# Seven units of an expert table fetched ahead of the first pass, and ten row products in the query stage

## The chip, the cores and the metric

The kernel runs as one program on 1 core of a Trainium2 chip. The metric is device time in microseconds (us), the median over runs; less is better. The kernel is written by hand for each engine: TensorE (PE, weight loads PEld), VectorE (DVE), ScalarE (ACT), GpSimd (POOL) and SyncE (SP). Each runs its own list of instructions in order and waits on semaphores. Transfers (DMA) are issued by SP, ACT and POOL on a queue each, and all run on the same 16 DMA engines.

## The reference

One layer of a transformer block on 256 tokens of width 2048, float32: a normalised input is projected (`w_in`), two attentions run beside each other, their outputs go through `w_o`, and then comes the part that this change is about:

```python
x = x + concat(A, B) @ w_o
h = rmsnorm(x)
qr = (h @ w_pq).reshape(b, t, 8, 2, 128)
sc = einsum('bthpd,hpnd->bthpn', qr, sub_keys)
s_top, i_top = top_k(sc, 16)
cand = s_top[..., 0, :, None] + s_top[..., 1, None, :]
c_top, c_pos = top_k(cand, 16)
expert = i0 * 128 + i1
a = gelu(einsum('bthkd,btd->bthk', u_tab[expert], h))
x = x + einsum('bthk,bthkd->btd', softmax(c_top) * a, v_tab[expert])
```

Each token picks 8 x 16 of 16384 experts; an expert is a row of 2048 numbers in the first table (`u_tab`) and one in the second (`v_tab`).

## The kernel before, in words

**Two ways of computing the experts.** The 128 later tokens take the dense way: TensorE multiplies all of `u_tab` in 128 units of 128 experts (1 MB each) with the tokens (`u_chunk`, L1597), the first pass; the results are gated by what each token picked, and a second pass multiplies them with the 128 units of `v_tab` (`v_chunk`, L1643). The 128 earlier tokens take the sparse way: for each of 128 picks POOL gathers one row of the table for each token (128 rows of 8 KB, 1 MB; "a row" below is such a gather) and VectorE multiplies it with the tokens (L1192) or adds it up weighted (L1201). There are 256 rows, first 128 of `u_tab`, then 128 of `v_tab`; gathers of the second table skip what has no weight.

**Stages, on the profile's clock.** Input projection and attentions to about 347 us; the output projection `w_o` in two groups of 16 loads, the second from about 350 to 408; the query stage (`w_pq`, 32 loads) to about 509; the first pass to 1016; the second pass to the end.

**Weights in two parts.** In the stages up to the queries each load of 0.5 MB comes into one of four raw buffers (SP, `load`, L383). ScalarE rounds its two halves (`split_hi`, L570), VectorE subtracts to get the low part of each half (`split_lo_half`, L877), and TensorE multiplies both parts. Four halves can be ahead of TensorE; a raw buffer is loaded again when its low parts are made. In the query stage a half is a low part of 128 x 512, there are 64, and TensorE's products with it are L1538, L1539 and L1543.

**Units of the first table.** Five units (0 to 4) are loaded by SP in the query stage, one after every fourth weight load (`first_unit`, L418), into places of `acts` that are free by then. The others go through a ring of four buffers: the even ones by SP (L436 to L446), the odd ones by ScalarE (`odd_unit`, L816), each when the unit that lay there has been used (`unit_used`). In the first pass the sums of a chunk go to ScalarE for the gelu (L783).

**Rows.** POOL's `gather(r)` (L525, L527) waits until the row's buffer has been used (`row_used`). The first `R_FRONT` = 8 rows turn through two buffers in the query stage; then there are six, from `R_MORE` on eight. `pool.memset` (L536) fills the place where gates will lie with ones; it waits until five units have been used, because units lie there, and the gathers behind it wait with it. VectorE's order is written out by hand: after the first head's `top_k` it makes four low parts, then a row product (L1241 to L1246); then the other heads with two rows each; in the gated half one row for each second chunk. The gate operands (`hots`, L1261) come behind the 46th row.

**Second pass.** Units 0 to 5 are loaded whole, the others gathered by POOL (L544) when the unit six before has been used, skipping experts that nobody used. After unit u POOL gathers rows up to `end`, a straight line over the units (L546). At the end VectorE makes the last row in four pieces (L1199), and adds up the outputs (L1350).

Of the kernel before, what the change touches and what calls it, by code (L numbers as in the profile page):

```python
# [18 lines left out]
def build_block(nc, io):  # L19
# [5 lines left out]
    ACT = mybir.ActivationFunctionType  # L25
# [43 lines left out]
    NRING, NROW = 4, 8  # L69
# [7 lines left out]
    with ExitStack() as ctx:  # L77
# [101 lines left out]
        x2n = [region(D * b, D) for b in range(TT)]  # L179
        A_QR = TT * D  # L180
        qr = region(A_QR, 16 * SEQ).rearrange("p (c t) -> p c t", c=16)
# [6 lines left out]
        first_units = [region(2 * UNIT * i, 2 * UNIT) for i in (0, 1, 4, 7, 5)]  # L188
# [60 lines left out]
        first_in = [sem(f"first_in{i}") for i in range(NRING + 1)]  # L249
# [94 lines left out]
        ROWS_U = 88  # L344
        R_FRONT, R_MORE, ROWS_PICKED = 8, 46, 39
# [5 lines left out]
        ROWS_SB = 81  # L351
# [24 lines left out]
        def _(sp):  # L376
# [26 lines left out]
            wo = io["w_o"].rearrange("(k p) n -> p k n", p=P)  # L403
            for group in range(2):
                with sp.Fori(0, D // 512) as n:
                    for j in range(4):
                        k = 8 * group + 2 * j
                        load(n * 4 + (B_WO + 16 * group + j), j, wo[:, k:k + 2, ds(n * 512, 512)])
            def u_unit(v):
                return io["u_tab"][ds(v * P, P), :]  # L410
# [6 lines left out]
            def first_unit(j):  # L417
                sp.dma_start(first_units[j], u_unit(j)).then_inc(first_in[j], 16)  # L418

            query_weights(0, 3)  # L420
            sp.wait_ge(piece_used, 2 * B_PQ + 2)
            first_unit(0)
            query_weights(3, 4)
            first_unit(1)
            query_weights(4, 5)
            first_unit(2)
            query_weights(5, 6)
            first_unit(3)
            query_weights(6, 7)
            sp.wait_ge(x2_stored, 16)  # L430
# [123 lines left out]
        def _(act):  # L554
# [1165 lines left out]
```

## Time and profile before

| what | value |
|---|---|
| median of 3 runs | 1521.25 us (1520.91 to 1523.61) |
| the profiled execution's own time | 1521.85 us |
| its span, first to last instruction | 1519.8 us |
| busy: TensorE, weight loads | 96%, 72% |
| busy: VectorE, ScalarE, GpSimd | 76%, 32%, 28% |
| moved by DMA | 516.25 MB, mean 340 GB/s |

A busy share is an average over stages with different limits: TensorE is near its pace everywhere, while the DMA engines are full in the later two thirds alone. So what one step costs is read from its own stretch: who was waited for there, and how long. Rows of a timeline give the start, the duration, engine, line, operation and tiles, how many were merged (x), and in brackets the idle time before and what ended it.

### The profile page before, as it was taken

The numbers are of one execution on the slowest core, as the hardware profiler recorded it, in microseconds if no ns is written. First come the engines' busy times: TensorE is split into PE (matmuls) and PEld (weight loads), VectorE is DVE, ScalarE is ACT, GpSimd is POOL, SyncE is SP. The second block draws the span as 40 slices with busy tenths as digits, with TensorE's granted clock in tenths as the row PEclk, the third lists the DMA queues.
The fourth block names the chain that finished last, engine by engine and source line by source line (L and its number), as shares of the span: only waits on it lengthen the run. The fifth ranks groups of instructions, "written<-read, shape, count | busy, mean of one in ns | idle before, by whom it ended". The sixth has DMA issues, their size and how long they took to land.

```text
span 1519.8 us, 21779 instructions
## 1 busy us (share of the span) xinstructions
PE 1451.8 (96%) x7977; PEld 1099.0 (72%) x7977; DVE 1154.4 (76%) x1797; ACT 487.8 (32%) x1402; POOL 430.5 (28%) x422
## 2 busy tenths in 40 slices
PE   8999999999999999999989999998897899999998
PEld 6767888888899999999989999983333343444443
DVE  5425688586687799999377777778766899998997
ACT  6646656764655200000134444457000000000000
POOL 2020000000001232222210111126444666665762
PEclk9999999999999999999999999999989999999999
DMA  9764544637669899999999999999999999999997
GB/s 348 277 139 111 163 134 139 206 131 240 205 232 407 335 398 422 421 422 421 422 421 421 422 422 416 403 414 417 419 416 417 404 392 398 398 412 352 382 408 281
DMA packets 115528, 516.25 MB, mean 340 GB/s; under 512 B 26112, under 2 KB 28288, under 8 KB 63312
## 3 DMA queue, kind: packets, MB, share of 16 engines
q0 software_dynamic: 57776, 294.93, 49.0%
q1 hardware_dynamic: 47888, 154.09, 27.9%
q10 hardware_dynamic: 9792, 66.35, 10.6%
q8 instruction: 35, 0.57, 0.2%
q14 instruction: 37, 0.30, 0.1%
HBM read 628.91 MB, written 3.41 MB: 416 GB/s over the span
## 4 chain that ended last, share of the span: by engine, by line
PE 53%; DMA 23%; DVE 16%; issue 4%; POOL 3%; ACT 1%; another core or an unknown queue 0%; POOLq 0%; ACTq 0%; SPq 0%; DVEq 0%
PE ps L1643 12%; PE ps L1597 12%; DMA acts<-in_v_tab,acts 8%; PE ps L1379 6%; PE ps L1384 6%; PE ps L1381 6%; DMA late<-in_u_rows,sel 6%; DVE late L1192 3%; DMA raw<-in_v_tab,acts 3%; DMA late<-in_v_tab,acts 3%; DVE ps L1201 2%; PE ps L1401 2%; PE ps L1543 2%; PE ps L1539 2%; PE ps L1538 2%
## 5 line engine op out<-in xcount | busy, mean ns | idle before, releaser
L877 DVE TENSOR_TENSOR w_lo<-raw,w_hi 128x512 fp32r<-128x512 f32 (+1 forms) x288 | 188.1, 682 | 129.7 <-ACT w_hi L570 127.7
L1597 PE MATMUL ps<-acts,late 128*128 128x128 f32 x1984 | 233.4, 277 | 7.3 <-DMA late<-in_u_tab 6.0
L1597 PEld LDWEIGHTS ps<-acts,late 128*128 128x128 f32 x1984 | 227.6, 193 | 10.8 <-ACT acts L783 5.7
L1597 PE MATMUL ps<-acts,raw 128*128 128x128 f32 x1952 | 228.7, 276 | 5.3 <-DMA raw<-in_u_tab 3.7
L1597 PEld LDWEIGHTS ps<-acts,raw 128*128 128x128 f32 x1952 | 222.1, 192 | 9.0 <-DMA raw<-in_u_tab 4.4
L570 ACT ACTIVATE w_hi<-raw 128x512 fp32r<-128x512 f32 (+1 forms) x288 | 170.2, 622 | 85.3 <-PE ps L1543 40.3
L1643 PE MATMUL ps<-raw,acts 128*128 128x512 f32 x352 | 161.8, 611 | 13.1 <-DMA raw<-in_v_tab,acts 10.7
L1643 PE MATMUL ps<-acts 128*128 128x512 f32 x336 | 156.9, 618 | 16.7 <-DMA acts<-in_v_tab,acts 15.5
L1201 DVE SCALAR_TENSOR_TENSOR ps<-acts,sel,ps 128x2048 f32<-128x2048 f32 x63 | 148.4, 2355 | 16.8 <-DMA acts<-in_v_tab,acts 9.4
L1201 DVE SCALAR_TENSOR_TENSOR ps<-late,sel,ps 128x2048 f32<-128x2048 f32 x63 | 148.4, 2355 | 15.2 <-DMA late<-in_v_tab,acts 7.9
L1643 PE MATMUL ps<-late,acts 128*128 128x512 f32 x336 | 150.3, 597 | 9.8 <-DMA late<-in_v_tab,acts 8.5
L1379 PE MATMUL ps<-w_hi,hT_hi 128*128 128x512 f32 (+1 forms) x448 | 148.9, 413 | 3.9 <-DVE hT_lo L890 3.2
L525 POOL DMA_INDIRECT acts<-in_u_rows,sel x62 | 72.8, 1174 | 265.7 <-DVE acts L1192 213.4
L525 POOL DMA_INDIRECT late<-in_u_rows,sel x66 | 79.2, 1199 | 238.5 <-DVE late L1192 218.4
L1643 PEld LDWEIGHTS ps<-raw,acts 128*128 128x128 f32 x352 | 67.4, 195 | 104.3 <-issue 83.1
L1643 PEld LDWEIGHTS ps<-acts 128*128 128x128 f32 x336 | 64.8, 197 | 106.0 <-issue 78.3
L1384 PE MATMUL ps<-w_lo,hT_hi 128*128 128x512 f32 (+1 forms) x448 | 137.5, 388 | 0.6 <-DVE w_lo L877 0.6
L1381 PE MATMUL ps<-w_hi,hT_lo 128*128 128x512 f32 (+1 forms) x448 | 137.7, 389 | 0.0
L1643 PEld LDWEIGHTS ps<-late,acts 128*128 128x128 f32 x336 | 62.3, 190 | 95.6 <-issue 74.3
L1192 DVE SCALAR_TENSOR_TENSOR late<-late,acts 128x2048 f32<-128x2048 f32 x43 | 97.7, 2287 | 26.8 <-DMA late<-in_u_rows,sel 26.6
L1379 PEld LDWEIGHTS ps<-w_hi,hT_hi 128*128 128x128 f32 x448 | 80.8, 190 | 25.2 <-issue 6.8
L1384 PEld LDWEIGHTS ps<-w_lo,hT_hi 128*128 128x128 f32 x448 | 84.2, 188 | 18.2 <-DVE w_lo L877 1.1
(225 smaller groups left out, 1958.0 us busy)
## 6 DMA issues: line engine op xcount, KB each, us to landing
raw<-in_w_in SPq DMA_DIRECT2D x72, 512.0 KB, 4.2
late<-in_u_tab SPq DMA_DIRECT2D x32, 1024.0 KB
raw<-in_u_tab SPq DMA_DIRECT2D x31, 1024.0 KB
raw<-in_u_tab ACTq DMA_DIRECT2D x30, 1024.0 KB
late<-in_u_tab ACTq DMA_DIRECT2D x30, 1024.0 KB
raw<-in_w_o SPq DMA_DIRECT2D x32, 512.0 KB, 4.3
raw<-in_w_pq SPq DMA_DIRECT2D x32, 512.0 KB, 4.7
acts<-in_u_tab SPq DMA_DIRECT2D x5, 1024.0 KB, 8.8
```

Of the source, the lines that this page charges most:

```text
L525: pool.indirect_dma_start(row[BUF[r]], None, io["u_rows"], bass.IndirectOffsetOnAxis(ap=idx[:, n:n + 1], axis=0)).then_inc(row_in[BUF[r]], 16)
L570: nc.scalar.activation(whi[(2 * j + half) % NPART][:, 0:w], raw[j % NRAW][:, half * w:half * w + w], ACT.Copy).then_inc(hi_done, 1)
L877: V.tensor_tensor(wlo[slot_no][:, 0:w], raw[j % NRAW][:, half * w:half * w + w], whi[slot_no][:, 0:w].bitcast(F32), ALU.subtract).then_inc ...
L1192: V.scalar_tensor_tensor(row[BUF[r]], row[BUF[r]], 1.0, held if moved else hs, ALU.mult, ALU.mult, accum_out=a_sel[:, n:n + 1]).then_inc(r ...
L1201: V.scalar_tensor_tensor(held, row[BUF[r]], w_sp[:, n:n + 1], acc if r == V_ROW[0] else held, ALU.mult, ALU.add).then_inc(row_used, 1)
L1379: mm(out[b], hT_hi[:, k, t[b]], whi[part][:, 0:w], start=start and kk == 0, stop=False)
L1381: mm(out[b], hT_lo[:, k, t[b]], whi[part][:, 0:w], start=False, stop=False)
L1384: ins = mm(out[b], hT_hi[:, k, t[b]], wlo[part][:, 0:w], start=False, stop=stop and kk == 1)
L1401: ins = mm(ps[:, bank, :], src[:, k, b * P:b * P + P], w[:, k, :], start=k == 0, stop=k == ks - 1)
L1538: mm(out, whi[piece % NPART][:, w], hT_hi[:, k, :], start=k == 0, stop=False)
L1597: ins = mm(ps[:, q, 0:N_DN], unit[:, k * P:k * P + P], hF[:, k, :], start=k == 0, stop=k == KD - 1)
L1643: ins = mm(out_bank(n), acts_c[i * V_FULL + q], ring[q][:, 512 * n:512 * n + 512], start=first, stop=last)
```

## The change

Seven units instead of five are loaded ahead. Units 0 to 4 go out in the second half of `w_o`: SP waits for the last value products (`y_mm`), then issues unit 0, and one more behind every fourth weight load. Units 5 and 6 follow in the query stage, where unit 6 waits for a copy that lay in its place. Units 8 and 9 go to the ring as soon as the raw buffers under it are free, 7 and 10 at the end of the stage. The room comes from the queries, which are now kept in a ring of four small places instead of 16, and from the squares' output, which is moved. The fill with ones waits for seven used units. VectorE makes three low parts between two row products instead of four, so ten rows instead of eight lie in the query stage, and all marks that count rows move by two. In the second pass the straight line for the rows is divided by 123 and not by 120, so that it no longer reaches the last row before the last unit.

```diff
-    NRING, NROW = 4, 8
+    NRING, NROW, N_FIRST = 4, 8, 7
...
-        x2n = [region(D * b, D) for b in range(TT)]
-        A_QR = TT * D
-        qr = region(A_QR, 16 * SEQ).rearrange("p (c t) -> p c t", c=16)
+        x2n = [region(A_HF + D * b, D) for b in range(TT)]
+        qr = [early[:, 256:512], early[:, 1024:1280], early[:, 1408:1664], gate_low[:, 0:SEQ]]
...
-        first_units = [region(2 * UNIT * i, 2 * UNIT) for i in (0, 1, 4, 7, 5)]
+        first_units = [region(2 * UNIT * i, 2 * UNIT) for i in (0, 1, 2, 3, 4, 7, 5)]
...
-        ROWS_U = 88
-        R_FRONT, R_MORE, ROWS_PICKED = 8, 46, 39
+        ROWS_U = 90
+        R_FRONT, R_MORE, ROWS_PICKED = 10, 48, 41
...
-        ROWS_SB = 81
+        ROWS_SB = 83
...
             for group in range(2):
-                with sp.Fori(0, D // 512) as n:
+                if group:
+                    sp.wait_ge(y_mm, 16)
+                    first_unit(0)
+                for n in range(D // 512):
                     for j in range(4):
                         k = 8 * group + 2 * j
-                        load(n * 4 + (B_WO + 16 * group + j), j, wo[:, k:k + 2, ds(n * 512, 512)])
+                        load(n * 4 + (B_WO + 16 * group + j), j, wo[:, k:k + 2, n * 512:n * 512 + 512])
+                    if group:
+                        first_unit(1 + n)
...
-            query_weights(0, 3)
-            sp.wait_ge(piece_used, 2 * B_PQ + 2)
-            first_unit(0)
-            query_weights(3, 4)
-            first_unit(1)
-            query_weights(4, 5)
-            first_unit(2)
-            query_weights(5, 6)
-            first_unit(3)
-            query_weights(6, 7)
+            query_weights(0, 2)
+            first_unit(5)
+            query_weights(2, 6)
             sp.wait_ge(x2_stored, 16)
             sp.wait_ge(xT_mm, KD)
-            first_unit(4)
-            query_weights(7, 8)
-
-            sp.wait_ge(lo_done, 2 * (B_U + 3) - 2 * (NRAW - 1))
-            sp.dma_start(ring[1], u_unit(NRING + 1)).then_inc(unit_in[1], 16)
+            first_unit(6)
+            query_weights(6, 8)
+
+            for j in range(2):
+                sp.wait_ge(lo_done, 2 * (B_U + 2 * j + 1) - 2 * (NRAW - 1))
+                sp.dma_start(ring[j], u_unit(2 * NRING + j)).then_inc(unit_in[j], 16)
             sp.wait_ge(piece_used, 2 * B_U)
-            for j in range(2, NRING):
-                sp.dma_start(ring[j], u_unit(NRING + j)).then_inc(unit_in[j], 16)
-            sp.dma_start(ring[0], u_unit(2 * NRING)).then_inc(unit_in[0], 16)
-            sp.wait_ge(unit_used, NRING + 3)
+            sp.dma_start(ring[3], u_unit(N_FIRST)).then_inc(unit_in[3], 16)
             sp.dma_start(ring[2], u_unit(2 * NRING + 2)).then_inc(unit_in[2], 16)
...
-            pool.wait_ge(unit_used, NRING + 1)
+            pool.wait_ge(unit_used, N_FIRST)
...
-                end = ROWS_U + (len(ROWS) - ROWS_U) * (u + 1 - V_FULL) // (NKEY - 2 - V_FULL)
+                end = ROWS_U + (len(ROWS) - ROWS_U) * (u + 1 - V_FULL) // (NKEY + 1 - V_FULL)
...
-                nc.scalar.activation(qr[:, c, :], ps[:, c % 2, 0:SEQ], ACT.Copy).then_inc(qr_done, 1)
+                if c >= 4:
+                    act.wait_ge(score_mm, TT * (c // 2 - 1))
+                nc.scalar.activation(qr[c % 4], ps[:, c % 2, 0:SEQ], ACT.Copy).then_inc(qr_done, 1)
...
-                if c % 2 and c > 3:
+                if c % 2 and c >= N_FIRST:
...
-                for _ in range(4):
+                for _ in range(3):
                     weights_low()
                 if rows_done[0] < R_FRONT - 1:
                     next_row()
...
-                early_unit = isinstance(i, int) and NRING * i + q <= NRING
+                early_unit = isinstance(i, int) and NRING * i + q < N_FIRST
```

## Rows read from the trace of the kernel before

**Rows 1.** Stretches: us, busy us (records) of each engine, granted clock, DMA share, GB/s.

```profile
455.00:500.00 45.00, 45.00 (x379) 45.00 (x379) 34.08 (x43) 23.33 (x44) 8.15 (x7) 1.00 0.98 392
...
510.00:533.00 23.00, 22.97 (x206) 22.81 (x206) 14.87 (x38) 3.87 (x9) 9.28 (x7) 1.00 0.99 407
533.00:545.00 12.00, 12.00 (x110) 12.00 (x109) 11.65 (x22) 0.83 (x3) 5.40 (x4) 1.00 0.93 359
545.00:775.00 230.00, 213.95 (x1842) 208.39 (x1842) 192.82 (x544) 21.53 (x69) 59.92 (x38) 1.00 1.01 422
775.00:930.00 155.00, 153.06 (x1330) 151.76 (x1330) 119.24 (x169) 74.25 (x221) 20.27 (x21) 0.99 1.01 421
...
1016.00:1175.00 159.00, 133.64 (x279) 55.00 (x280) 116.37 (x122) 39.56 (x252) 82.81 (x83) 0.94 1.02 418
1175.00:1370.00 195.00, 185.69 (x424) 78.39 (x423) 174.58 (x79) 0.22 (x1) 127.15 (x128) 1.00 1.01 401
1370.00:1500.00 130.00, 126.16 (x289) 54.73 (x288) 118.41 (x51) 0.00 (x0) 81.93 (x83) 0.99 0.98 383
```

**Rows 2.** Timeline of ScalarE, output projection: start, us, what, idle time before.

```profile
346.12 0.39 ACT L638 ACTIVATE hT_hi<-ps 128x256 fp32r<-128x256 f32 x1 [2.17 <-PE ps L1454]
...
359.39 1.15 ACT L570 ACTIVATE w_hi<-raw 128x512 fp32r<-128x512 f32 x2 [4.46 <-DMA raw<-in_w_o]
360.76 1.88 ACT L570 ACTIVATE w_hi<-raw 128x512 fp32r<-128x512 f32 x3 [0.22 <-DMA raw<-in_w_o]
```

**Rows 3.** Timeline of TensorE, output projection and end of the query stage.

```profile
360.07 0.73 PE L1379 MATMUL ps<-w_hi,hT_hi 128*128 128x512 f32 x2 [0.37 <-ACT w_hi L570]
362.95 0.62 PE L1379 MATMUL ps<-w_hi,hT_hi 128*128 128x512 f32 x2
...
508.17 0.64 PE L1543 MATMUL ps<-hT_hi,w_lo 128*128 128x256 f32 x4
```

**Rows 4.** Timeline of GpSimd in the query stage: two gathers of rows.

```profile
464.56 1.14 POOL L525 DMA_INDIRECT acts<-in_u_rows,sel  x1 [6.81 <-DVE acts L1192]
...
496.57 1.15 POOL L525 DMA_INDIRECT acts<-in_u_rows,sel  x1 [6.04 <-DVE acts L1192]
```

**Rows 5.** Timeline of VectorE in the query stage: L877 low part, L1192 product.

```profile
459.89 0.69 DVE L877 TENSOR_TENSOR w_lo<-raw,w_hi 128x512 fp32r<-128x512 f32 x1 [0.68 <-ACT w_hi L570]
...
462.00 2.28 DVE L1192 SCALAR_TENSOR_TENSOR acts<-acts 128x2048 f32<-128x2048 f32 x1
...
474.41 2.29 DVE L1192 SCALAR_TENSOR_TENSOR acts<-acts 128x2048 f32<-128x2048 f32 x1
```

**Rows 6.** Stretch of one us behind the last gather's data in the query stage.

```profile
502.00:503.00 1.00, 1.00 (x11) 1.00 (x10) 0.85 (x3) 0.79 (x2) 0.00 (x0) 1.00 0.00 0
```

**Rows 7.** Timeline of GpSimd, head of the first pass: gathers and the fill.

```profile
515.50 0.94 POOL L525 DMA_INDIRECT acts<-in_u_rows,sel  x1 [0.30 <-issue]
528.64 6.93 POOL L536 MEMSET acts<- 128x8192 f32 x1 [12.20 <-PE ps L1597]
535.72 0.95 POOL L525 DMA_INDIRECT late<-in_u_rows,sel  x1
```

**Rows 8.** Timeline of VectorE in the first pass: two row products.

```profile
519.88 2.29 DVE L1192 SCALAR_TENSOR_TENSOR late<-late,acts 128x2048 f32<-128x2048 f32 x1 [5.01 <-DMA late<-in_u_rows,sel]
...
767.17 2.29 DVE L1192 SCALAR_TENSOR_TENSOR late<-late,acts 128x2048 f32<-128x2048 f32 x1 [4.84 <-DMA late<-in_u_rows,sel]
```

**Rows 9.** Timeline of TensorE in the first pass: the first gate group.

```profile
774.53 1.22 PE L1613 MATMUL ps<-hot_a 128*128 128x256 f32 x4 [6.00 <-ACT hot_a L795]
```

**Rows 10.** Timeline of GpSimd at the end: last row's and last unit's gathers.

```profile
1492.22 0.99 POOL L527 DMA_INDIRECT acts<-in_v_tab,acts  x1 [0.30 <-issue]
...
1495.64 0.99 POOL L544 DMA_INDIRECT raw<-in_v_tab,acts  x1 [1.13 <-PE ps L1643]
```

**Rows 11.** Timeline of TensorE at the end: the last two chunks.

```profile
1509.32 7.13 PE L1643 MATMUL ps<-raw,acts 128*128 128x512 f32 x16 [0.62 <-DMA raw<-in_v_tab,acts]
```

**Rows 12.** Timeline of VectorE at the end: the last row in four pieces.

```profile
1508.73 2.72 DVE L1199 SCALAR_TENSOR_TENSOR acts<-acts,sel,ps 128x512 f32<-128x512 f32 x4
```

More of the change, by code:

```diff
@@ L248, in build_block @@
         unit_in = [sem(f"unit_in{i}") for i in range(V_FULL)]
-        first_in = [sem(f"first_in{i}") for i in range(NRING + 1)]
+        first_in = [sem(f"first_in{i}") for i in range(N_FIRST)]
         value_in = [sem(f"value_in{i}") for i in range(V_FULL)]
@@ L403, in _, with u_unit, first_unit @@
             wo = io["w_o"].rearrange("(k p) n -> p k n", p=P)
+            def u_unit(v):
+                return io["u_tab"][ds(v * P, P), :]
+            def first_unit(j):
+                sp.dma_start(first_units[j], u_unit(j)).then_inc(first_in[j], 16)
             for group in range(2):
-                with sp.Fori(0, D // 512) as n:
+                if group:
+                    sp.wait_ge(y_mm, 16)
+                    first_unit(0)
+                for n in range(D // 512):
                     for j in range(4):
                         k = 8 * group + 2 * j
-                        load(n * 4 + (B_WO + 16 * group + j), j, wo[:, k:k + 2, ds(n * 512, 512)])
-            def u_unit(v):
-                return io["u_tab"][ds(v * P, P), :]
+                        load(n * 4 + (B_WO + 16 * group + j), j, wo[:, k:k + 2, n * 512:n * 512 + 512])
+                    if group:
+                        first_unit(1 + n)
             def query_weights(first, end):
@@ L415, in query_weights @@
                         load(i * 4 + (B_PQ + j), j, io["w_pq"][ds(i * (4 * P) + j * P, P), :])
-            def first_unit(j):
-                sp.dma_start(first_units[j], u_unit(j)).then_inc(first_in[j], 16)
-            query_weights(0, 3)
-            sp.wait_ge(piece_used, 2 * B_PQ + 2)
-            first_unit(0)
-            query_weights(3, 4)
-            first_unit(1)
-            query_weights(4, 5)
-            first_unit(2)
-            query_weights(5, 6)
-            first_unit(3)
-            query_weights(6, 7)
+            query_weights(0, 2)
+            first_unit(5)
+            query_weights(2, 6)
             sp.wait_ge(x2_stored, 16)
             sp.wait_ge(xT_mm, KD)
-            first_unit(4)
-            query_weights(7, 8)
-            sp.wait_ge(lo_done, 2 * (B_U + 3) - 2 * (NRAW - 1))
-            sp.dma_start(ring[1], u_unit(NRING + 1)).then_inc(unit_in[1], 16)
+            first_unit(6)
[3 more added lines that the diff above has]
+                sp.dma_start(ring[j], u_unit(2 * NRING + j)).then_inc(unit_in[j], 16)
             sp.wait_ge(piece_used, 2 * B_U)
-            for j in range(2, NRING):
-                sp.dma_start(ring[j], u_unit(NRING + j)).then_inc(unit_in[j], 16)
-            sp.dma_start(ring[0], u_unit(2 * NRING)).then_inc(unit_in[0], 16)
-            sp.wait_ge(unit_used, NRING + 3)
+            sp.dma_start(ring[3], u_unit(N_FIRST)).then_inc(unit_in[3], 16)
             sp.dma_start(ring[2], u_unit(2 * NRING + 2)).then_inc(unit_in[2], 16)
@@ L1558, in head_scores @@
                         c = 2 * hp + i
-                        ins = mm(ps[:, 2 + g % 4, i * P:i * P + P], qr[:, c, b * P:b * P + P], subk[:, c, :], start=True, stop=True)
+                        ins = mm(ps[:, 2 + g % 4, i * P:i * P + P], qr[c % 4][:, b * P:b * P + P], subk[:, c, :], start=True, stop=True)
                     ins.then_inc(score_mm, 1)
@@ L1587, in u_chunk @@
                     pe.wait_ge(score_done, 2 * NH)
-                early_unit = isinstance(i, int) and NRING * i + q <= NRING
+                early_unit = isinstance(i, int) and NRING * i + q < N_FIRST
                 if early_unit:
                     pe.wait_ge(first_in[NRING * i + q], 16)
-                elif q:
+                elif q == NRING - 1:
                     pe.wait_ge(unit_in[q], i * 16)
@@ L1638, in v_chunk @@
                 if isinstance(i, int) and i == 0:
-                    pe.wait_ge(unit_in[q], 16 * (NKEY // NRING - (q == 0)) if q < NRING else 16)
+                    pe.wait_ge(unit_in[q], 16 * (NKEY // NRING - (q < NRING - 1)) if q < NRING else 16)
                 else:
```

## The prediction

> **What bounds the kernel now.** I read the page first, then the stretches by stage, the timelines around the places that the change touches, and the end. By stretches [rows 1] TensorE is never idle from 455 to 500 us, the query stage, and idles 16.1 of 230 us in the first half of the first pass (545 to 775), 25.4 of 159 at the head of the second pass and 9.3 of the next 195. Over the same stretches the DMA engines show a share of about 1.0 and 401 to 422 GB/s: from 545 us on, what is fetched sets the pace, and TensorE stands only where a fetch is late. So a megabyte fetched earlier pays only if the engines would else have been idle, and a megabyte (1.05 MB) costs 2.5 us at 418 to 422 GB/s. In the query stage the engines show 0.98 and 392 GB/s, but nobody there waits for them.
>
> **The sum** is made against the profiled execution, 1521.85 us (span 1519.8 and 2.05 around it); the median of the runs is 0.6 lower. What a measurement can tell from no change is about 0.2%, 3.0 us.
>
> **Five units in the second half of the output projection.** Unit 0 now goes out on SP's queue between the sixteenth and the seventeenth of 32 weight loads, behind a new wait for the last of the 16 value products. ScalarE copies that product at 346.12 [rows 2], before SP has issued the sixteenth load, so the wait itself costs nothing; queued behind it are all later weight loads. The sixteenth load is late already: ScalarE stood 4.46 us for it at 359.39, and had the seventeenth at 360.76 [rows 2], because POOL has three transfers in flight there. TensorE restarts at 360.07 on the sixteenth and comes to the seventeenth at 362.95 [rows 3]; its first rounded part was there at 361.4 (360.76 + 0.63): a slack of 1.5 us. One unit ahead in the same queue delays it 2.5. I take **+1.0**, between 0 and 2.5; a gain is excluded, since nothing is taken away here. Units 1 to 4 follow after each fourth load, where ScalarE waits for TensorE and not for a fetch; they are hidden by the four raw buffers.
>
> **Query stage: three low parts between two row products, ten rows.** VectorE works in order, so a row product that waits for its gather holds back the low parts that TensorE needs. There are two row buffers: a gather is issued 0.28 us after the product that frees its buffer (a product starts at 462.00 and takes 2.28, the gather goes out at 464.56 [rows 4, 5]), and the second product after that needs it. The trip from issue to data is not shown. Its bounds: the gather of 496.57 moved its megabyte alone and the engines fell silent at 502 [rows 4, 6], 5.8 us with 0.4 for the signal (my estimate); the gather of 464.56, with weights beside it, served at 474.41 a product that did not wait [rows 5], so at most 9.85. I take 8.4: the lone trip, and 2.6 more because weights take turns with the row (another megabyte at 407 GB/s). Before, eight low parts fitted between a gather's two products and hid it (12.4 us from 462.00 to 474.41); six do not. One turn of both buffers is then 2.28 + 0.28 + 8.4 = 10.96 us for two rows. The first product comes one low part earlier, at 460.6 (459.89 + 0.69 [rows 5]); the ninth row starts four turns later, at 504.4; with its product and four low parts of 0.69 the last low part is ready at 509.5. TensorE wants it at 508.2 [rows 3]. **+1.3**; with 5.8 it is 0, with 9.85 it is +7.1. A gain is excluded: TensorE has no idle time to lose there. Two unit loads instead of five stand beside the weights, which helps nobody who waits.
>
> The Trainium skill, DMA: Bandwidth & Descriptors, "Anatomy of one DMA", gives a transfer issued from GpSimd about 2.0 us and its bytes at 436 GB/s. For a row that is an estimate of 4.4 us alone, against 5.8 here, and with the same 2.6 for company the term would be 0 and the sum 1.3 lower. The trace disagrees with it by 1.4 us, and its row is what I use.
>
> **First pass, first half.** TensorE takes 3.57 us a chunk (206 records in 22.97 us, 32 to a chunk [rows 1]) and did not wait for its first twelve, so units fetched earlier save nothing there. They save later: two units fewer to move in the saturated stretch, 2 x 2.5 = 5.0 us less. But a ring of four buffers and six row buffers cannot take what comes next any sooner. At the start of the pass, about 510.4, what is asked for is three units less what has come of one, and six rows: some 9 MB, moved at 407 GB/s by 532. The next unit goes out when the eighth chunk is used (510.4 + 8 x 3.57 = 539), as before. The next rows wait for POOL's fill of the ones: its wait moves from five chunks used to seven, because the units now lie where it writes. It started at 528.64 and took 6.93, and the next gather came at 535.72, 20 us after the last one [rows 7]. Queued behind that wait are all later gathers, and VectorE waits for them; now they come at 542.9. So the engines stand about 8.5 us (532 to 539, and some of what follows the lone unit), where before they were at 359 GB/s for 12 us, worth 1.8 [rows 1]. That gives back 7 of those us. **+2.0** net, between -5.0 (the lead is kept) and +7.1 (the rows' delay is paid in full). What is late next is the rows: VectorE's product at 767.17 waits 4.84 for its row, and TensorE stands 6.00 at 774.53 for the gate operands that follow from it [rows 8, 9].
>
> **Second half of the first pass:** the same chunks and rows, 0; TensorE idles 1.9 us there from 775 to 930, so at most -1.9 [rows 1].
>
> **Second pass.** Two rows of the first table fewer are left for its saturated head: 2 x 2.5 = **-5.0** (between 0 and that). The formula that spreads the rows over the units falls from 168/120 = 1.40 to 166/123 = 1.35 rows a unit. From 1175 to 1370, 195 us at 401 GB/s moved 78.2 MB for 53 chunks (424 records, eight each) and 79 products [rows 1]: 0.59 MB each if all were alike, 1.48 us. Over 53 chunks 53 x 0.05 = 2.7 transfers fewer: **-3.9**, between 0 and -9.3, the whole idle time of TensorE there. They move to the end, where the engines show 0.98 or less. **The tail:** the last row's gather stood 3.42 us ahead of the last unit's (1492.22, 1495.64 [rows 10]); now two rows come behind it, 1.3 and 2.6 later. The last unit was used 13.7 us after its issue (1509.32 [rows 11]); with the same trip the last row lands near 1512, and its four pieces (2.72 [rows 12]), behind the product before it, end near 1515.5 instead of 1511.4, where VectorE already has the final sums to make: **+1.0**, between 0 and 2.6.
>
> At nothing: the four-buffer ring of queries (ScalarE's new wait is for scores made a whole pair earlier), the moved squares, the unrolled loop, SP's issues of 0.33 us on a queue that mostly waits.
>
> Sum: 1.0 + 1.3 + 2.0 - 5.0 - 3.9 + 1.0 = -3.6, so 1518.2 on the profiled execution and **1517.6** on the median.
>
> **Rivals.** (A) *Slower: the row's round trip.* If two buffers can't turn as fast as the low parts are wanted, TensorE waits in the query stage. It begins to cost at a trip of 8.1 us and makes the kernel slower than before from 9.3. With units in its way a first row of the first pass came 10.8 us after 509.1 (product at 519.88 behind a wait of 5.01 [rows 8]; TensorE's last part ends the stage there); then a turn is 13.36, the term 10.9, the sum +6.0: 1527.3. For it: the units 6 and 8 still cross this stage. Against it: no product waited before. (B) *No change: the rows hold the gate.* The row stream runs without a gap from 535.72 to the product at 767.17, 32 rows, 7.2 us each. If it only starts 7.1 later and keeps that pace, the gate is 7.1 later whatever TensorE has in hand: the term is +7.1, the sum +1.5, 1522.7. Against it: TensorE's lead leaves room on the engines. The Trainium skill, same page, "Queues, rings and completion order", says that each engine goes round the queues that have work; by that rule the rows get no more than their turn as long as both unit queues are busy, which is this case; the trace's steady 7.2 us agrees. (C) *More: the lead is kept*, the term is -5.0, the sum -10.6, 1510.6. For it: the engines are full for 222 us after; against it the ring that can't take more.
>
> **Chances.** The forecast 0.42, A 0.15, B 0.20, C 0.18, something else 0.05. Below 1518.2 counts as faster: C, and six tenths of the forecast's own spread, 0.46; within 0.2%: most of B and a third of the forecast, 0.35; slower: most of A and what is left of B, 0.19. The range goes from C to A, 1510 to 1527; the forecast's own is 1514 to 1522.
>
> **What would show it.** Right: in the query stage VectorE's row products wait for their gathers and TensorE loses some 1 to 2 us; the engines' GB/s fall between 532 and 543; the product ahead of the gate comes some 4 us later than 767; the second pass is 8 us shorter. Wrong: TensorE idle for 5 us or more before 510 (A), or a gate earlier than 767 (C).

## The result and the profile after

| kernel | median | runs | ratio to before, 95% interval |
|---|---|---|---|
| before | 1520.9 us | 14 | 1 |
| changed | 1526.53 us | 14 | 1.0031 [1.0024, 1.0038] |

The change makes the kernel slower by 0.31%, some 4.7 us of 1521 (the two medians are 5.6 apart, which the interval takes in). The profiled execution took 1524.17 us (span 1522.2), the fastest of the 14 runs of the changed kernel. So its trace shows the cheap end of the losses; other traces further down, in which the same part of the program ran, show the dearer end.

The same stretches as in [rows 1], with the output projection's second half ahead of them:

```profile
347.00:410.00 63.00, 62.66 (x293) 51.99 (x292) 39.97 (x65) 35.26 (x69) 1.58 (x3) 1.00 0.86 308
...
455.00:500.00 45.00, 42.63 (x352) 42.00 (x352) 32.76 (x41) 20.62 (x40) 9.32 (x8) 1.00 0.92 349
500.00:510.00 10.00, 9.17 (x75) 8.77 (x74) 8.55 (x11) 4.24 (x9) 1.15 (x1) 1.00 0.91 347
510.00:533.00 23.00, 22.53 (x200) 22.32 (x199) 18.28 (x59) 4.36 (x10) 7.44 (x6) 1.00 0.95 378
533.00:545.00 12.00, 12.00 (x110) 12.00 (x109) 11.62 (x25) 0.84 (x4) 5.10 (x1) 1.00 0.27 89
...
1016.00:1175.00 159.00, 136.13 (x335) 59.51 (x334) 115.37 (x122) 42.94 (x263) 80.35 (x81) 0.96 1.02 418
1175.00:1370.00 195.00, 188.91 (x435) 81.32 (x434) 172.85 (x78) 0.21 (x1) 128.11 (x128) 1.00 1.01 400
1370.00:1500.00 130.00, 127.44 (x295) 55.03 (x294) 117.18 (x50) 0.00 (x0) 82.30 (x84) 1.00 1.00 391
```

Three things stand out. TensorE, which never waited from 455 to 500 us, now idles 2.4 us there. From 533 to 545 the DMA engines move 89 GB/s where they moved 359. And TensorE idles less in the second pass (6.1 against 9.3 us from 1175 to 1370), although the kernel ends later. In the projection nothing is lost: 62.66 us of 63 busy with the five unit loads among the weights.

**The query stage.** The chain of waits in this stretch (start, us, what) alternates between VectorE and the fetch of a row:

```profile
456.33 10.11 DMA acts<-in_u_rows,sel
466.46 2.31 DVE acts L1191 x2
468.78 0.26 issue
469.04 8.75 DMA acts<-in_u_rows,sel
477.81 2.31 DVE acts L1191 x2
...
480.38 8.72 DMA acts<-in_u_rows,sel
489.12 2.31 DVE acts L1191 x2
...
491.69 8.02 DMA acts<-in_u_rows,sel
499.74 2.30 DVE acts L1191 x2
502.04 0.61 DVE w_lo L876
502.69 0.74 PE ps L1542 x4
```

This is the turn of two buffers that the prediction wrote down: product 2.3, issue 0.26, trip 8.0 to 10.1. These are trips that a product waited for; the product of 493.15 did not wait for its row, and the tenth row's trip, 10.8 us, holds back no low part. The low parts that VectorE makes meanwhile do not appear, since they are hidden beside the trips. What TensorE sees of it (timeline, idle time before in brackets) are four waits for low parts, 3.2 us together, and a last low part that it multiplies at 512.55 instead of 508.17 [rows 3]:

```profile
487.17 0.74 PE L1542 MATMUL ps<-hT_hi,w_lo 128*128 128x256 f32 x4 [1.84 <-DVE w_lo L876]
...
502.69 0.74 PE L1542 MATMUL ps<-hT_hi,w_lo 128*128 128x256 f32 x4 [0.83 <-DVE w_lo L876]
...
508.14 0.74 PE L1542 MATMUL ps<-hT_hi,w_lo 128*128 128x256 f32 x4
...
509.68 0.64 PE L1542 MATMUL ps<-hT_hi,w_lo 128*128 128x256 f32 x4
...
511.12 0.64 PE L1542 MATMUL ps<-hT_hi,w_lo 128*128 128x256 f32 x4
...
512.55 0.64 PE L1542 MATMUL ps<-hT_hi,w_lo 128*128 128x256 f32 x4
```

**The fill.** GpSimd's timeline at the head of the first pass, to be laid beside [rows 7]:

```profile
521.49 0.94 POOL L522 DMA_INDIRECT acts<-in_u_rows,sel  x1 [0.30 <-issue]
539.90 6.93 POOL L533 MEMSET acts<- 128x8192 f32 x1 [17.47 <-PE ps L1596]
546.98 0.95 POOL L522 DMA_INDIRECT late<-in_u_rows,sel  x1 [0.15 <-issue]
```

The first gather behind the fill goes out at 546.98 instead of 535.72: 6.9 us because the fill waits for two more chunks (it starts 25.2 us after the first chunk instead of 18.4), and 4.4 because the pass began later. This is the hole of 89 GB/s. The row ahead of the gate and the gate itself (VectorE's and TensorE's timelines; [rows 8, 9] are the same before) come 6.8 later:

```profile
773.98 2.29 DVE L1191 SCALAR_TENSOR_TENSOR late<-late,acts 128x2048 f32<-128x2048 f32 x1 [5.03 <-DMA late<-in_u_rows,sel]
```
```profile
781.34 1.22 PE L1612 MATMUL ps<-hot_a 128*128 128x256 f32 x4 [6.82 <-ACT hot_a L794]
```

**The end.** TensorE's last two chunks, then VectorE's last rows and its final sums (the counterparts of [rows 11, 12]):

```profile
1502.85 7.16 PE L1642 MATMUL ps<-raw,acts 128*128 128x512 f32 x16
```
```profile
1511.45 2.35 DVE L1200 SCALAR_TENSOR_TENSOR ps<-late,sel,ps 128x2048 f32<-128x2048 f32 x1
1513.91 2.72 DVE L1198 SCALAR_TENSOR_TENSOR acts<-late,sel,ps 128x512 f32<-128x512 f32 x4
1516.55 2.47 DVE L1349 TENSOR_TENSOR acts<-ps,acts 128x512 f32<-128x512 f32 x4
```

Before, VectorE had its last row at 1511.45 (1508.73 + 2.72 [rows 12]) and waited 2.53 us for TensorE before the sums:

```profile
1513.98 1.48 DVE L1350 TENSOR_TENSOR acts<-ps,acts 128x512 f32<-128x512 f32 x2 [2.53 <-PE ps L1643]
```

Now TensorE is done at 1510.0 and everything waits for VectorE's rows, which end at 1516.6. The bound of the end has changed sides.

**Stage by stage**, from the starts that the timelines give (first gather of the query stage; first chunk of the first pass; first chunk of the second; end of the span):

| from, to | before | after | difference | forecast |
|---|---|---|---|---|
| start to first gather | 452.42 | 452.27 | -0.2 | +1.0 |
| first gather to first chunk | 57.86 | 62.39 | +4.5 | +1.3 |
| first chunk to second pass | 506.04 | 508.75 | +2.7 | +2.0 |
| second pass to the end | 503.53 | 498.76 | -4.8 | -7.9 |
| sum | 1519.85 | 1522.17 | +2.3 | -3.6 |

So in these two profiles two terms are far off: the query stage, 3.2 us too small, and the second pass with its tail, 3.1 us too good. Where the passes part differs from profile to profile: the first pass, the same program in the changed kernel and in runs 3 and 11 further down, took 508.75, 507.61 and 503.57 us. So the experiments are read by their ratios first.

### The profile page after: what moved, and what is told of

The parts are those of the page before. It is cut to its first block, busy times and chain, and to the rows that moved or that the text cites. A ratio compares the mean times of both kernels' runs of the same rounds, so it can differ in the third digit from the quotient of the medians.

```text
span 1522.2 us, 21734 instructions
## 1 busy us (share of the span) xinstructions
PE 1450.5 (95%) x7977; PEld 1100.9 (72%) x7977; DVE 1151.6 (76%) x1797; ACT 487.6 (32%) x1402; POOL 430.2 (28%) x422
## 4 chain that ended last, share of the span: by engine, by line
PE 52%; DMA 25%; DVE 17%; issue 2%; POOL 2%; ACT 1%; DVEq 0%; POOLq 0%; ACTq 0%; SPq 0%
PE ps L1642 13%; PE ps L1596 12%; DMA late<-in_u_rows,sel 6%; PE ps L1378 6%; PE ps L1383 6%; PE ps L1380 6%; DMA raw<-in_v_tab,acts 5%; DMA late<-in_v_tab,acts 5%; DMA acts<-in_v_tab,acts 3%; DVE late L1191 3%; DVE ps L1200 2%; DMA acts<-in_u_rows,sel 2%; PE ps L1400 2%; DVE acts L1191 2%; DMA raw<-in_u_tab 2%
## 5 line engine op out<-in xcount | busy, mean ns | idle before, releaser
L1642 PE MATMUL ps<-acts 128*128 128x512 f32 x336 | 151.4, 601 | 8.5 <-DMA acts<-in_v_tab,acts 7.4
L1191 DVE SCALAR_TENSOR_TENSOR acts<-acts 128x2048 f32<-128x2048 f32 x40 | 91.0, 2287 | 25.1 <-DMA acts<-in_u_rows,sel 25.0
```

The costliest lines, as they stand in the source:

```text
L1191: V.scalar_tensor_tensor(row[BUF[r]], row[BUF[r]], 1.0, held if moved else hs, ALU.mult, ALU.mult, accum_out=a_sel[:, n:n + 1]).then_inc(r ...
L1642: ins = mm(out_bank(n), acts_c[i * V_FULL + q], ring[q][:, 512 * n:512 * n + 512], start=first, stop=last)
```

## The experiments

All times are medians; each run's ratio is to the kernel before on the same chip. "The changed kernel" is 1.0031. In the table behind the last run, "PE" and "rows" are the ends of TensorE's last chunk and of VectorE's last row, counted from the start of the second pass.

**1. Four low parts again, ten rows kept.**

```diff
-                for _ in range(3):
+                for _ in range(4):
                     weights_low()
```

> Ten rows in the query stage as in the changed kernel, but four low parts between two row products, as before; the last two products then come behind the last low part. Theory (two row buffers cannot turn in 8 to 10 us with only six low parts between; TensorE paid 4.3 us for it): the first chunk of the first pass starts near 510.4 again instead of 514.66, TensorE shows no wait for a low part after 460, and the kernel is 3.5 to 4.5 us faster than the changed one, near 1522. Rival (the two extra products are VectorE work that has to be done before the picks of the last head, or the two ring units loaded in the stage hold the weights up): the first chunk stays at 513 or later, or it comes at 510.4 and the row ahead of the gate is as late as before, so that the gate stays at 782 and the time within 1 us of 1526.5.

1519.8 us, 0.9986 [0.9977, 0.9995]: 0.45% under the changed kernel, and a little faster than before. From the first gather to the first chunk it takes 57.87 us. VectorE's timeline shows where the last two rows went:

```profile
503.37 2.29 DVE L1191 SCALAR_TENSOR_TENSOR acts<-acts 128x2048 f32<-128x2048 f32 x1
...
507.40 2.29 DVE L1191 SCALAR_TENSOR_TENSOR acts<-acts 128x2048 f32<-128x2048 f32 x1 [1.74 <-DMA acts<-in_u_rows,sel]
...
514.08 2.29 DVE L1191 SCALAR_TENSOR_TENSOR acts<-acts 128x2048 f32<-128x2048 f32 x1 [4.39 <-DMA acts<-in_u_rows,sel]
```

VectorE waits for both, 1.74 and 4.39 us, but no low part stands behind them any more, so TensorE does not. The theory holds; the gain is 6.8 us where 3.5 to 4.5 was expected. Part of that is the cheap profile from which the expectation was made; the rest, about a microsecond, is within the intervals and stays open.

**2. The fill behind four used units.** Other places for the units: those under the fill are used as chunks 1 to 3.

```diff
-        first_units = [region(2 * UNIT * i, 2 * UNIT) for i in (0, 1, 2, 3, 4, 7, 5)]
+        first_units = [region(2 * UNIT * i, 2 * UNIT) for i in (0, 5, 7, 4, 1, 2, 3)]
-                        first_unit(1 + n)
+                        first_unit((4, 5, 6, 3)[n])
-            first_unit(5)
+            first_unit(2)
-            first_unit(6)
+            first_unit(1)
-            pool.wait_ge(unit_used, N_FIRST)
+            pool.wait_ge(unit_used, 4)
```

> The changed kernel with the seven units placed so that the four that lie outside chunk results and under the fill with ones are used first: the fill waits for four used units instead of seven. Theory (the rows hold the gate and the fill holds the rows): the fill starts near 529.2 instead of 539.9, the first gather behind it goes out near 536.2 instead of 546.98, the engines' GB/s between 533 and 545 rise from 89 to over 300, TensorE comes to the gated chunks 4 to 8 us earlier than 782.4, and the kernel is 3 to 7 us faster than the changed one. Rival (the DMA engines are full until 930, so rows that come earlier make units late by as much): TensorE waits longer for units before chunk 67, the gated chunks come less than 2 us earlier, and the time is within 1.5 us of 1526.5.

1521.32 us, 0.9995 [0.9986, 1.0004]: 0.36%, 5.5 us, under the changed kernel. GpSimd's timeline and the stretch from 533 to 545:

```profile
532.18 6.93 POOL L533 MEMSET acts<- 128x8192 f32 x1 [9.30 <-PE ps L1596]
539.26 0.94 POOL L522 DMA_INDIRECT late<-in_u_rows,sel  x1
```
```profile
533.00:545.00 12.00, 12.00 (x110) 12.00 (x109) 11.58 (x26) 0.83 (x3) 7.99 (x3) 1.00 0.65 250
```

In this run the pass began 2 us later than in the changed kernel's profile, at 516.63, yet the gather behind the fill goes out 7.7 us earlier, and the first pass takes 502.34 us instead of 508.75. So here the late fill is a loss of its own, nearly as large as the query stage's. The edit also changes the order in which the units are loaded, which no run separates from the fill. The GB/s rose less than expected, 250 and not over 300; the gated chunks come 3.1 us earlier on the clock (779.27 against 782.36) and 5.1 counted from the start of the pass.

**3. The old divisor.**

```diff
-... // (NKEY + 1 - V_FULL)
+... // (NKEY - 2 - V_FULL)
```

> The changed kernel with the straight line of the second pass divided by 120 again (1.38 rows a unit instead of 1.35). Theory (in the changed kernel TensorE is done at 1510 and VectorE adds rows until 1516.6, so the rows now come too late and the tail is VectorE's): VectorE's last row ends 3 to 6 us earlier than 1516.6, TensorE's last chunk ends 3 to 6 us later than 1510.0, and the kernel is 1 to 3 us faster than the changed one. Rival (the smaller slope is what the second pass gains by): TensorE's last chunk ends 6 us or more later than 1510.0 and the kernel is as slow as the changed one or slower by up to 4 us.

1526.63 us, 1.0027 [1.0018, 1.0037]: the same as the changed kernel. TensorE's last chunk ends 496.4 us after the start of the second pass instead of 486.6, VectorE's last row 491.3 instead of 493.2. The divisor moves 9.8 us of TensorE's time and 1.9 of VectorE's, where the theory had 3 to 6 of each. So the end passes from VectorE back to TensorE, as the theory says, but too far for a gain: the rival's time. (The second pass starts at different times in the two; counted from the first chunk of the first pass it is 8.6 and 3.1.)

**4. Small rows in the query stage.**

```diff
+                if kind == "u" and 2 <= r < R_FRONT:
+                    pool.indirect_dma_start(row[BUF[r]][:, 0:512], None, io["u_rows"].rearrange("n (q d) -> (n q) d", q=4), ...)
```

> The changed kernel, where the third to tenth gather of the query stage fetch 2 KB for each token instead of 8 KB (it leaves out three quarters of those rows, and reads others; the products are as long as before). Only the stage's end is read. Theory (the round trip of a row holds VectorE, and VectorE the low parts): the trips fall from 8.0 to 10.8 us to 4 to 6, VectorE's products from the third on do not wait, and the first chunk starts at 510.4 to 511.5 instead of 514.66. Rival (VectorE has too much work in the stage, two more products of 2.3 us): the products do not wait, and the first chunk still starts at 513.5 or later.

From the first gather (453.78) to the first chunk (511.65) it takes 57.87 us, within 0.01 us the time of before; no product from the third on waits. VectorE does the same ten products and low parts in the same order. So its work is not the cause, the trip is.

**5. Both edits, four low parts and the early fill** (the diffs of 1 and 2).

> The two edits together: four low parts between two row products, and the fill waiting for four used units. Theory (two separate losses: TensorE waits in the query stage, and the DMA engines stand idle behind the fill): the query stage takes 57.9 us from its first gather to the first chunk, the first gather behind the fill goes out near 532 instead of 542.5, the engines' GB/s between 533 and 545 rise from 115 over 300, and the time is 3 to 6 us under the 1519.8 of the four low parts alone, 1514 to 1517. Rival (with four low parts rows and units are late together already, TensorE did not wait at the gate any more, so an earlier row only makes a unit later): within 1.5 us of 1519.8.

1518.35 us, 0.9979 [0.9969, 0.9990]. Against the four low parts alone (0.9986 [0.9977, 0.9995]) the intervals overlap: the expected 3 to 6 us are not there. GpSimd's and VectorE's timelines tell why:

```profile
524.19 6.92 POOL L533 MEMSET acts<- 128x8192 f32 x1 [4.94 <-PE ps L1596]
536.93 2.24 POOL L522 DMA_INDIRECT late<-in_u_rows,sel  x1 [5.82 <-DVE late L1191]
```
```profile
524.16 6.98 DVE L1169 TENSOR_SCALAR acts<-acts 128x16 uint32<-128x16 uint32 x1
533.86 2.28 DVE L1191 SCALAR_TENSOR_TENSOR late<-late,acts 128x2048 f32<-128x2048 f32 x1
```

The fill is done at 531.1, 11.2 us earlier than in run 1, but the next gather needs a buffer that VectorE has not used yet, and goes out at 536.93. VectorE is late because two row products now lie ahead of its picks (as in run 1), and because an instruction on 128x16 numbers took 6.98 us while the fill ran. In run 1 the fill held such an instruction for 6.44 us as well, but there VectorE had made the pair of products of 525.38 and 527.59 by then:

```profile
535.92 6.44 DVE L1168 TENSOR_SCALAR acts<-acts 128x16 uint32<-128x16 uint32 x1
```

In run 5 the hold lies ahead of the pair that frees the gather's buffer. What the fill held back, VectorE now holds.

**6. Both edits with the divisor 121.**

```diff
-... // (NKEY + 1 - V_FULL)
+... // (NKEY - 1 - V_FULL)
```

> As the two edits together, with the straight line of the second pass divided by 121 instead of 123. Theory (with 123 VectorE's rows end last, with 120 TensorE's chunks; between them both end together): TensorE's last chunk ends 5 to 8 us later than with 123, counted from the start of the second pass, VectorE's last row 1 to 2 us earlier, and the time is 0.5 to 1.5 us less than that of the two edits with 123. Rival (the divisor moves nothing at all, since all that is fetched must be fetched by the end): within 0.5 us, and VectorE's last row ends as before.

1514.95 us, 0.9954 [0.9941, 0.9968], the lowest median of all here (runs 10 and 12 come within its interval): 6.5 us under the 1521.45 of the kernel before on the same chip, and 3.4 under the same with 123. TensorE ends 492.7 after the start of the pass, VectorE's rows 491.6: the two ends meet. TensorE's end moved by 3.5 us where 5 to 8 were expected, VectorE's by 4.2 where 1 to 2 were, so the theory holds in its direction and not in its sizes.

```profile
1500.30 7.34 PE L1642 MATMUL ps<-raw,acts 128*128 128x512 f32 x16
```
```profile
1503.88 2.72 DVE L1198 SCALAR_TENSOR_TENSOR acts<-late,sel,ps 128x512 f32<-128x512 f32 x4
1506.51 2.47 DVE L1349 TENSOR_TENSOR acts<-ps,acts 128x512 f32<-128x512 f32 x4
```

**7. Units and divisor without the rows.**

```diff
-        ROWS_U = 90
-        R_FRONT, R_MORE, ROWS_PICKED = 10, 48, 41
+        ROWS_U = 88
+        R_FRONT, R_MORE, ROWS_PICKED = 8, 46, 39
-        ROWS_SB = 83
+        ROWS_SB = 81
-                for _ in range(3):
+                for _ in range(4):
```

> The changed kernel with the rows as they were before: eight rows in the query stage, four low parts between two, all marks back by two; the seven units ahead, the late fill and the divisor 123 stay. Theory (units ahead save two megabytes in the saturated stretch, 5 us, and the later fill gives that back; the two extra rows are worth their 2 megabytes, since they were fetched when the engines were partly idle): query stage 57.9 us, the row ahead of the gate some 5 to 7 us later than before's 767, and 1521 to 1524, no better than before, and 2 to 4 us more than the ten rows with four low parts (1519.8). Rival (the two rows in front are worth nothing and the units give all): within 1 us of 1519.8.

1525.66 us, 1.0027 [1.0018, 1.0036]. No wait in the query stage (57.86), and still 0.27% slower than before, more than the 1521 to 1524 expected: the rest of the change loses by itself. The ten rows with four low parts (run 1) are worth 0.41% of it.

**8 to 12. The parts alone, in the kernel before.** Run 8 changes only the divisor, to 123:

> The kernel before with the divisor 123 in place of 120 and nothing else: the change's third part alone. Theory (with 123 the rows come so late that VectorE ends the kernel): counted from the start of the second pass, VectorE's last row ends 3 to 7 us later than before's 495.1 and TensorE's last chunk 5 to 9 us earlier than its 500.1; the kernel is 0 to 4 us slower than before, 1521 to 1525. Rival (the prediction's own term: fewer rows beside the units, and VectorE catches up): 3 to 5 us faster than before, 1516 to 1518.

1523.74 us, 1.0008 [1.0000, 1.0017]. TensorE's last chunk comes 493.4 after the start of the pass instead of 500.1, VectorE's last row 500.0 instead of 495.1:

```profile
1502.62 7.15 PE L1643 MATMUL ps<-raw,acts 128*128 128x512 f32 x16
```
```profile
1513.69 2.72 DVE L1199 SCALAR_TENSOR_TENSOR acts<-acts,sel,ps 128x512 f32<-128x512 f32 x4
1516.33 2.48 DVE L1350 TENSOR_TENSOR acts<-ps,acts 128x512 f32<-128x512 f32 x4
```

TensorE's 6.7 us are bought with 4.9 us of VectorE's, and VectorE's are the ones that count. Run 9 changes only the rows, as the change does (the marks forward by two, `range(4)` to `range(3)`):

> The kernel before with ten rows and three low parts between two products, five units loaded in the query stage and divisor 120 as before: the change's second part alone. Theory (the wait for rows is all of the loss, the seven units ahead are worth next to nothing): from the first gather to the first chunk 62.4 to 64.5 us instead of 57.9, and the time as with all but the divisor, 1525 to 1528. Rival (the units ahead pay for part of it, or their absence from the query stage shortens the trips): 1529 or more, with a stage of 66 us or more. Second rival (the two rows pay for the wait): 1521 to 1523.

1524.49 us, 1.0017 [1.0008, 1.0026], with 64.59 us from the first gather to the first chunk: the longest of all, in a profile that is the slowest execution of this kernel (1528.77). The median stands between the theory and the second rival; two rows less to fetch later pay for most of the wait, not for all. Run 10 takes the marks, keeps four low parts, and sets 121; run 12 takes the marks alone; run 11 is the changed kernel with 121.

> The kernel before with ten rows, four low parts between two products as before, and divisor 121; no unit is loaded earlier. Theory (the seven units ahead are worth next to nothing, since what they save was hidden or comes back as a later fill): 1515 to 1518, within 2 us of the 1514.95 of the version with seven units, early fill and 121. Rival (the units are worth their two megabytes, 5 us, once nothing else is in the way): 1519 to 1521.

> The changed kernel with 121 in place of 123, and nothing else. Theory (the tail is VectorE's at 123 and TensorE's at 120, and both end together at 121): VectorE's last row ends 2 to 4 us earlier, counted from the start of the second pass, TensorE's last chunk 3 to 6 us later, and the kernel is 2 to 4 us faster than the changed one, 1522.5 to 1524.5. Rival (what the run with four low parts and early fill showed at 121 needs their lead in rows): within 1 us of 1526.5.

> The kernel before with ten rows in the query stage, four low parts between two products, and nothing else: units as before, divisor 120. Theory (two rows fetched where the engines are partly idle are two megabytes less where they are full, 2 x 2.5 us): 57.9 us from the first gather to the first chunk, and 1516 to 1518. Rival (the divisor 121 made most of the gain of the version with 121): 1519.5 or more, with TensorE's last chunk behind VectorE's last row by 4 us or more.

| run | units | rows, low parts | divisor | fill waits for | first gather to first chunk | PE | rows | ratio |
|---|---|---|---|---|---|---|---|---|
| before | 5 | 8, four | 120 | 5 | 57.86 | 500.1 | 495.1 | 1 |
| changed | 7 | 10, three | 123 | 7 | 62.39 | 486.6 | 493.2 | 1.0031 |
| 1 | 7 | 10, four | 123 | 7 | 57.87 | 488.8 | 495.4 | 0.9986 |
| 2 | 7 | 10, three | 123 | 4 | 63.34 | 488.2 | 494.8 | 0.9995 |
| 3 | 7 | 10, three | 120 | 7 | 64.43 | 496.4 | 491.3 | 1.0027 |
| 5 | 7 | 10, four | 123 | 4 | 57.87 | 489.2 | 495.8 | 0.9979 |
| 6 | 7 | 10, four | 121 | 4 | 57.87 | 492.7 | 491.6 | 0.9954 |
| 7 | 7 | 8, four | 123 | 7 | 57.86 | 495.4 | 502.0 | 1.0027 |
| 8 | 5 | 8, four | 123 | 5 | 57.87 | 493.4 | 500.0 | 1.0008 |
| 9 | 5 | 10, three | 120 | 5 | 64.59 | 498.8 | 492.9 | 1.0017 |
| 10 | 5 | 10, four | 121 | 5 | 57.87 | 494.3 | 493.3 | 0.9962 [0.9949, 0.9974] |
| 11 | 7 | 10, three | 121 | 7 | 62.62 | 497.1 | 496.0 | 1.0019 [1.0011, 1.0028] |
| 12 | 5 | 10, four | 120 | 5 | 57.87 | 497.8 | 492.7 | 0.9965 [0.9951, 0.9978] |

Run 12 (1516.79 us) gains 5.3 us by marks moved by two and nothing else; run 10 (1515.77) adds 121 and gains nothing clear on that, and run 6 adds units and early fill and again nothing clear. Both times are as expected. Between run 9 and run 12 stands one edit, `range(3)` for `range(4)`, and 0.52%, 7.9 us; no unit is loaded earlier in either, so the price of three low parts is not that of the units. Run 11 (1523.83) is 1.8 us under the changed kernel by the ratios; their intervals overlap. Its time lies in the expected range, its ends do not: counted from the start of the second pass VectorE's rows end 2.8 us later and not 2 to 4 earlier, TensorE 10.5 later and not 3 to 6. Its first pass was 5.2 us shorter; counted from the first chunk of that pass the rows end 2.4 earlier and TensorE 5.3 later.

## Why the prediction was wrong, point by point

The sum had the kernel 3.6 us faster, and it is 4.7 slower. The time lies near the end of rival A, 1527.3, but A needed trips of 10.8 us in every turn, and the trips that held low parts back took 8.0 to 10.1: the loss came another way.

**The projection, +1.0.** Right that it is small: it cost nothing that shows. TensorE is busy for 62.66 of 63 us there, and the first gather of the query stage came at 452.27 instead of 452.42.

**The query stage, +1.3: the first of two steps that failed.** The mechanism was right (row products that wait hold the low parts back), and so was the turn: trips of 8.0 to 10.1 us against 8.4, and the ninth product at 505.19 against 504.4 forecast:

```profile
505.19 2.29 DVE L1191 SCALAR_TENSOR_TENSOR acts<-acts 128x2048 f32<-128x2048 f32 x1 [1.34 <-DMA acts<-in_u_rows,sel]
...
507.40 2.49 DVE L876 TENSOR_TENSOR w_lo<-raw,w_hi 128x512 fp32r<-128x512 f32 x4
```

Wrong was the sentence that the last of the four low parts behind it is ready at 509.5 and wanted at 508.2. The four stand behind the product together, and TensorE wants the first of them three halves earlier. It takes 1.44 us for a half (509.68 to 511.12 above), so 508.17 - 3 x 1.44 = 503.9, and the timeline of before has it there:

```profile
503.85 0.64 PE L1543 MATMUL ps<-hT_hi,w_lo 128*128 128x256 f32 x4
```

With the forecast's own 504.4 that first low part is ready at 504.4 + 2.28 + 0.69 = 507.4: 3.5 late, not 1.3. With the 505.19 of the trace it is 508.1 and 4.2 late; the stage lost 4.5. The loss did not arise at the ninth product alone: TensorE's waits of 1.84 us at 487.17 and 0.83 at 502.69 lie ahead of it, each on the first low part behind a product; what the ninth shows is the state at the end. The other profiles in which three low parts and full rows ran (runs 2, 3, 9 and 11) lost 4.8 to 6.7. Rival A, whose range of prices this falls into, had its threshold from the same wrong comparison: by the first low part the loss begins at a trip of 7.5 us, and at 8.1 it is already some 2.3 us.

The estimate of 4.4 us for a lone row from the figures of the Trainium skill (DMA: Bandwidth & Descriptors, "Anatomy of one DMA") stays under what the traces show. In run 1 the gather of 501.67 serves at 507.40 a product that waited for it, 5.7 us. The prediction's bound of 5.8 is the nearer one. Neither row was alone from start to end: packets of other loads ran beside both in part.

**The first pass, +2.0.** Right in mechanism: the fill waits for seven chunks, and all later gathers wait behind it. In the net it is about right too, but not by the +2.7 of the one profile, since the first pass alone varies by more. Two pairs of runs differ in the units and the fill alone, and over both passes together they show +1.9 us (run 3, 1007.39, against run 9, 1005.53) and +2.7 (run 7, 1013.60, against run 8, 1010.89). The 5.0 saved and the 7 given back, from which the +2.0 was netted, do not show one by one: run 2 gives back 5.5 us by an earlier fill, but with four low parts (run 5 against run 1) the same edit gives nothing clear. So that the net came right may be luck. That rows are what is late next also held: TensorE stood 6.82 us at the gate, with the product ahead of it 6.8 later than before. Of that delay 4.4 is the later start of the pass. The stream did not keep its 7.2 us a row, as rival B had it: 32 rows from 546.98 to 773.98 are 7.09 each, and so it made up 4.5 of the 11.3 it started late.

**The units themselves.** The forecast had two more units ahead save 5.0 us in the saturated stretch and lose them to the fill. No such saving shows: run 6 against run 10, where the fill waits for four and five units, shows no clear difference, and run 7 against run 8 (seven units with a fill behind seven, against five) is 0.19% slower.

**Two rows fewer in the second pass, -5.0.** Right in size: run 12 does this alone and gains 0.35%, 5.3 us. In its profile 2.8 us of that lie in the first pass (503.22 against 506.04) and 2.3 in the second, where the forecast had put it all.

**The divisor, -3.9, and the tail, +1.0: the second step that failed.** Alone in the kernel before (run 8) 123 gives +0.08%, not a gain, and taking it back in the changed kernel (run 3) changes nothing clear: 1.0027 against 1.0031. TensorE did become faster by what was forecast and more. But rows that end at 1515.5 cost only +1.0 if TensorE still ends at its old 1516.45 (1509.32 + 7.13 [rows 11]) and VectorE has time in hand before the final sums; the same sum had just moved TensorE's end 8.9 us forward. Two engines end this kernel, and the later one sets the time. The forecast's own 1515.5, with the 5.5 us that the profile after has from there to the end of the span (1516.63 to 1522.17), makes 1521.0, later than before's 1519.8. What remained of the gain is what VectorE's rows gained. Runs 3, 5, 6 and 8 show both sides: at 120 TensorE ends last, at 123 VectorE, and at 121 they end 1.1 us apart. Of these steps only the one from 123 to 121 with early rows (run 5 to run 6, 3.4 us) is clear of the noise.

**The sum.** With the measured 4.5 and -4.8 in place of these two steps it is 1.0 + 4.5 + 2.0 - 4.8 = +2.7, beside +2.3 in the profiled execution. The 4.7 of the ratio are more, in part because that execution was a cheap one: over the five profiles with three low parts and full rows the query stage took 63.47 us on average, 5.6 more than before. Where the remaining us or so lies, and why the stage takes 62.4 us in one execution and 64.6 in another, no run here settles. Nor was it tried whether a third row buffer would let ten rows and three low parts run without a wait.

## What to carry to other kernels

Work queued behind a wait is late from its first piece on: compare the first thing that the consumer wants from it, not the last. Where two engines finish a kernel, carry both ends through the sum and take the later one; a gain for one of them ends where the other stands, and a knob that shifts work between them gains only until they meet (from 123 to 121 here, with the rows in front and four low parts; from 120 to 121 nothing clear). And before fetching something earlier, look who waits for the place it will occupy: seven megabytes ahead instead of five brought nothing clear even with an early fill, and cost 0.19% where the fill under them came later by two chunks, while two rows put where the engines had gaps brought 5 us.

## What the runs showed of the hardware that was not expected

A fill on GpSimd can stop VectorE. In the changed kernel the same copy of 128x256 takes 0.29 us ahead of the fill of 539.90 and 3.50 us during it, ending a little after the fill does:

```profile
529.98 0.29 DVE L1145 COPY acts<-acts 128x256 f32<-128x256 f32 x1
...
541.26 2.29 DVE L1191 SCALAR_TENSOR_TENSOR late<-late,acts 128x2048 f32<-128x2048 f32 x1
...
543.48 3.50 DVE L1145 COPY acts<-acts 128x256 f32<-128x256 f32 x1
```

The row product of 541.26, with two inputs from SBUF (the on-chip buffer), is not touched: 2.29 us, as anywhere. In run 5 an instruction on 128x16 was held for 6.98 us, which is the whole fill, and in run 1 for 6.44. The Trainium skill says so (SBUF — State Buffer, "Who interferes with whom"): copies, casts and tensor_scalar can take the port pair that VectorE shares with GpSimd, and of two that want it the second blocks until the other instruction is done; an instruction with two inputs from SBUF collides only with a GpSimd instruction that reads. The traces agree, for these kinds and for the product that passes. So a fill has two prices, the gathers queued behind it and up to 7 us of VectorE, and it matters what VectorE still has to make: in run 1 the hold came behind the pair of row products, in run 5 ahead of it.
